# Four experts with a fixed place instead of three, and another order of the blocks, in a two-part transformer kernel

## What is computed

```python
scores = jax.nn.sigmoid(jnp.dot(h, w_router, preferred_element_type=F32))     # 256 x 64
...
_, idx = lax.top_k(jnp.where(expert_mask, biased, -jnp.inf), TOP_K)            # 8 of 64 experts a token
gate = gate / jnp.sum(gate, axis=-1, keepdims=True) * ROUTED_SCALE
...
y = (jax.nn.silu(xb @ w_gate[e]) * (xb @ w_up[e])) @ w_down[e]                 # 1024 -> 256 -> 1024
return y.astype(F32) * w_b[:, None]
```

## Time and profile before

| | us |
|---|---|
| median of three runs | 1319.2 |
| lowest and highest | 1319.04, 1322.58 |
| the profiled execution | 1320.62 |
| its span (first to last instruction) | 1318.8 |
| TensorE busy | 1273.8 (97%) |
| weight loads of TensorE | 796.1 (60%) |
| DVE, ACT, POOL busy | 778.5, 328.0, 147.7 |
| HBM read | 353.73 MB |

### The profile page before, as it was taken

How to read it: one execution, slowest core, us unless ns; L and a number is a source line. 1 busy time by engine, 2 the same in 40 slices (tenths; PEclk the granted TensorE clock), 3 DMA queues, 4 the chain that set the end, 5 groups by cost and what they waited for, 6 DMA issues and landing times.

```text
span 1318.8 us, 20435 instructions
## 1 busy us (share of the span) xinstructions
PE 1273.8 (97%) x7816; PEld 796.1 (60%) x7840; DVE 778.5 (59%) x1404; ACT 328.0 (25%) x658; POOL 147.7 (11%) x133
## 2 busy tenths in 40 slices
PE   9999999999999999999999999999999989999996
PEld 8667675875879566686686765744434434444431
DVE  1235589778789668968878574634444433444432
ACT  2144311201211251110122152322222222222221
POOL 1125500000011332000000902000000000000000
PEclk9999999999999999999999999999999999999998
DMA  9941154654533346675673414599999999999995
GB/s 380 363 157 35 65 192 164 250 225 174 206 128 130 133 187 234 251 304 209 261 301 147 163 62 178 220 421 410 420 420 421 420 422 420 421 420 421 420 421 236
DMA packets 51221, 356.48 MB, mean 270 GB/s; under 512 B 5936, under 2 KB 6208, under 8 KB 9536
## 3 DMA queue, kind: packets, MB, share of 16 engines
q1 hardware_dynamic: 45456, 321.45, 60.5%
q0 software_dynamic: 5392, 32.05, 6.6%
q10 hardware_dynamic: 288, 1.80, 0.3%
HBM read 353.73 MB, written 1.05 MB: 269 GB/s over the span
## 4 chain that ended last, share of the span: by engine, by line
PE 83%; DMA 6%; DVE 6%; SPq 2%; issue 2%; ACT 1%; DVEq 0%; ACTq 0%
PE ps L1094 14%; PE ps L1085 13%; PE ps L1637 11%; PE ps L1666 5%; PE ps L1567 4%; PE ps L861 4%; PE ps L1375 4%; PE ps L1617 4%; PE ps L1042 4%; DMA y_rows<-in_stream 3%; DMA ring<-in_stream 3%; PE ps L944 2%; PE ps L1024 2%; SPq L745 2%; PE ps L1368 2%; PE ps L965 2%
## 5 line engine op out<-in xcount | busy, mean ns | idle before, releaser
L1809 ACT ACTIVATE x_rows<-masked_and_probs 128x1024 bf16<-128x1024 f32 x72 | 76.1, 1057 | 243.0 <-DVE masked_and_probs L3146 175.4
L3146 DVE SCALAR_TENSOR_TENSOR masked_and_probs<-ps,small,gate_rows 128x512 f32<-128x512 f32 x48 | 33.8, 746 | 113.5 <-PE ps L1666 113.5
L1809 ACT ACTIVATE qk_tiles<-ps 128x512 f32<-128x512 f32 (+7 forms) x58 | 30.2, 522 | 256.4 <-PE ps L1085 248.4
L1085 PEld LDWEIGHTS ps<-xT,ring 128*128 128x128 f32 x768 | 87.7, 192 | 4.9 <-issue 4.9
L1085 PE MATMUL ps<-xT,ring 128*128 128x128 f32 x768 | 88.8, 275 | 0.8 <-issue 0.8
L1094 PE MATMUL ps<-ring,qk_tiles 128*128 128x512 f32 x192 | 85.2, 592 | 0.0
L3153 DVE TENSOR_TENSOR masked_and_probs<-masked_and_probs,x_rows 128x1024 f32<-128x1024 f32 x48 | 58.7, 1223 | 41.3 <-ACT x_rows L1809 41.3
L1637 PE MATMUL ps<-ring,vec_rows 128*32 128x512 f32 (+2 forms) x312 | 64.9, 592 | 4.0 <-DMA ring<-in_stream 2.7
L1617 PE MATMUL ps<-x_rows,probT 128*128 128x512 bf16 x264 | 61.1, 379 | 2.0 <-ACT x_rows L1809 0.8
L1567 PE MATMUL ps<-masked_and_probs,mix_rows 128*128 128x256 bf16 (+1 forms) x384 | 61.9, 269 | 0.7 <-ACT v_rows L2152 0.7
L1841 ACT ACTIVATE masked_and_probs<-masked_and_probs,negmax 128x128 f32<-128x128 f32 (+2 forms) x96 | 47.6, 497 | 59.8 <-DVE negmax L2403 52.5
(11 more groups left out here) (557 smaller groups left out, 2664.7 us busy)
## 6 DMA issues: line engine op xcount, KB each, us to landing
ring<-in_stream SPq DMA_DIRECT2D x201, 1024.0 KB, 10.1
qk_tiles<-in_stream SPq DMA_DIRECT2D x38, 1024.0 KB, 25.1
v_rows<-in_ada POOLq DMA_DIRECT2D x12, 1024.0 KB, 5.4
qk_tiles<-in_ada POOLq DMA_DIRECT2D x12, 1024.0 KB, 6.0
vec_rows<-in_stream SPq DMA_DIRECT2D x12, 1024.0 KB, 22.2
par<-in_stream SPq DMA_DIRECT2D x12, 1024.0 KB, 18.7
y_rows<-in_stream SPq DMA_DIRECT2D x12, 1024.0 KB, 20.7
xT<-in_stream SPq DMA_DIRECT2D x12, 1024.0 KB, 22.3
```

Source lines behind the costliest of these rows:

```text
L1085: mm = pe.matmul(ps[:, bank, m * P:(m + 1) * P], weights[:, kk, m * P:(m + 1) * P], tokens[:, kk, :], start=fresh and m == 0 and kk == 0, ...
L1809: return act.activation(dst, src, ACT.Copy, **kw)
```

## The change

One more expert (number 60) gets a fixed place of 96 rows. The places in sum are the same: 60 in 25 blocks, 4 + 3 + 3 + 17 + 33 instead of 3 + 3 + 3 + 19 + 32. Loads 0 to 11, not 0 to 8, are issued ahead of the wait for `s_sched`. One P block becomes an F block, and the order of the blocks is another one.

```diff
-FIXED = 3
+FIXED = 4
 UNIT = 32
 PER_MORE = P // UNIT
-WIDTHS = ((3 * P // 4, FIXED), (P, 3), (3 * P // 4, 3), (P // 2, 19), (P // 4, 32))
+WIDTHS = ((3 * P // 4, FIXED), (P, 3), (3 * P // 4, 3), (P // 2, 17), (P // 4, 33))
...
-BLOCKS = "TFQFPQPFSPPQQMMSPPQPPSQPM"
+BLOCKS = "FQFPFQSFPQPPPMMSQSPPMQQTP"
```

## The result

| | before | after |
|---|---|---|
| median of 12 runs, us | 1320.33 | 1325.06 |
| lowest and highest | 1318.37, 1322.58 | 1323.71, 1326.92 |
| ratio, 95% interval | | 1.0032 (1.0024 to 1.0040) |
| the profiled execution | 1320.62 | 1326.92 |
| its span | 1318.8 | 1325.1 |

The kernel is slower by 4.2 us (3.2 to 5.3). That is just over the 0.3% at which a change counts as seen. Single executions scatter by some 2 us, and the profiled one of after was the slowest of its twelve, so its 6.3 us over the profiled one of before is on the high side. What one trace shows is therefore read for its places, and the timed medians for the sizes.

The account below looks back on a forecast made before the run. The stream of 192 loads of 1 MB, coupled to TensorE by 17 buffers, was taken as the bound. 7.6 us gained by the preload less 10.9 us lost in holes gave +3.3 on 1319.2, so 1322.5 us; range 1318.5 to 1326.5.

Parts of the forecast that it names:

- the start of the sum: Whole kernel: the median before the change, 1319.2 us, to which the forecast added 3.3 us.
- rival 2: From block 1's wait on: TensorE's clock falls and the stream runs dry again; +5.2 us, 1324.4; chance 0.32.
- The likeliest case: Load stream to load 187: preload gain lost in later holes, then no further gap; +2.2 to +3.9 us; chance 0.5.
- the buffers swallow the gain: Block 0: only 21 loads can be issued by 875, engines idle from 872 until load 21 goes at 875.46.
- net term of +3.3 us: Stream up to load 187: 7.6 us gained from the preload, 10.9 us lost again in holes behind it.
- the bound of +2.6: Stream's pace up to load 187: 0.7 us less than +3.3 if the 0.8 us of old stops is taken out.
- does it run without a gap?: Block 1 on: TensorE waits 4.0 us for load 22, yet the stream keeps 0.9 us of cover at load 31.
- Rival 1, the gain stays: Load stream: its end moves with its earlier start; 7.6 us less, 1311.6 us; chance 0.08.
- Rival 3, a shorter wait in the loop: Loop's second half: short wait, clock stays up, 2.3 us of the tail go; 1321.2 us; chance 0.1.
- The end of the schedule: Closing blocks Q, Q, T, P: TensorE 2.8 us later at the loop's second half, still waits 5.6 us; hidden.
- The rule on early transfers: Loads ahead of the schedule: by issuing early alone, three loads are worth 7.6 us; it ignores buffers running out.

Follow-up runs that it names:

- e1: Changed kernel with 9 loads ahead of the schedule instead of 12, its new order and places kept; +1.5 us against the kernel before.
- e7: Kernel before with only its first two blocks exchanged, F ahead of T; +2.6 us against the kernel before.
- e3: Changed kernel with 9 loads ahead and the old order of blocks (T first, block 10 an F), so new places only; +0.8 us against the kernel before.
- e4: Changed kernel with four more matmuls, result unused, in TensorE's wait for load 22 in block 1; +2.9 us against the kernel before.
- e5: Kernel before with 16 buffers for the experts' loads instead of 17; +2.5 us against the kernel before.
- e9: Kernel before with 6 loads ahead of the schedule instead of 9; +6.9 us against the kernel before.
- e2: Changed kernel with 12 loads ahead kept but the old order of blocks (T first, block 10 an F); +9.8 us against the kernel before.
- e6: Changed kernel with 16 buffers for the experts' loads instead of 17; +9.5 us against the kernel before.

## Why the prediction came out as it did

**The end.** Forecast 1322.5 us (+3.3), range 1318.5 to 1326.5; measured 1325.06. The range held. Of the 2.6 us between 1322.5 and 1325.06, 1.1 are the start of the sum: the three runs of before had a median of 1319.2, the twelve 1320.33. The ratio's +4.2 us lies between the forecast (+3.3) and rival 2 (+5.2), and its interval, 3.2 to 5.3, holds both, so the time alone does not tell them apart. The trace does: the clock fell and the stream stumbled near 902 and 953, which are rival 2's signs. The likeliest case, at 0.5, had neither; rival 2 had 0.32. The range held because it was wide enough for both.

**Holds: the buffers swallow the gain.** Reckoned were 21 loads by 875, load 21 at 875.46 with the engines idle from 872; it went at 875.67, idle from 873. Reckoned was a net term of +3.3 us. The runs that have that hole alone gave +1.5 (e1) and +2.6 (e7). Their own traces can be read too, from block 0's start to the landing of load 187: 437.6 us in before, 440.1 in e1 and 440.6 in e7, so 2.5 and 3.0 more. (e3, which has no such hole, has 438.9: single traces scatter by about as much as that.) The term was rather too big, though 3.3 lies inside e7's interval. Its mechanism held, and the size is nearer to the bound of +2.6 that the prediction gave for a pace without the old stops: in e1 load 21 landed at 879.4 and load 187 at 1296.4, 2.512 us a load and not 2.517. Why the time of e1 is lower still stays open; e1 and e7 differ in everything behind the first block, and their intervals overlap.

**Failed: "does it run without a gap?"** This step answered that 0.9 us of cover was left in block 1. The wait it named was right, 4.0 us reckoned and 4.14 found. What it lacked was a fallen clock, which it left to rival 2, and the clock fell: 5.12 us for the half, a stumble at 902, one at 953. The forecast added nothing for this step. By e4 the clock's share is 1.3 us; rival 2 had 1.9 for it, a little high.

Could have told it? They had two waits: one of 5.24 us in which the clock fell, one of 2.71 us in which it did not. The length of the wait alone does not decide between such cases, as other traces of this study show:

```profile
911.22 1.03 PE L1666 MATMUL ps<-con,probT 128*32 128x512 f32 x1 [2.62 <-DMA ring<-in_stream]
...
1071.70 0.62 PE L1639 MATMUL ps<-ring,vec_rows 128*32 128x512 f32 x2 [3.19 <-DMA ring<-in_stream]
```

The first is e5: within a wait of 2.62 us the clock fell (0.84 over 910 to 911, 0.50 behind it, and the first record takes 1.03 us). The second is e3: through 3.19 us it stayed at 1.00. In e9 a wait of 4.13 us ended at full clock, and the clock fell 0.9 us behind it. But all of the 21 waits of 3.8 us or more in the stretch of the experts, over the eleven traces, have the low clock in them or within 1 us behind them. So a wait of 4 us deserved more than the 0.32 of rival 2; from the two waits of the earlier trace rows alone it could only be guessed.

**Where the rest is.** The changed kernel's +4.2 less the +1.5 of e1 is 2.7 us, which is what the three loads ahead cost in the new order. Of that, e4 gives 1.3 us to the clock. Of the other 1.4 the dip near 951 that is left in e4 is 0.7 us, by its two slices (270 and 262 GB/s for 420). It goes with the wait itself: TensorE is 4 us later from block 1 on, and e1, without that wait, has no dip there. The last 0.7 us are inside the intervals, and no run gives them a place.

**Rival 1, the gain stays,** fell in e2, e6 and in the changed kernel. **Rival 3, a shorter wait in the loop,** didn't come about: it was 5.8 us, reckoned 5.6.

**The end of the schedule** was foreseen to be hidden. The waits ahead of the loop are 21.7 - 5.8 = 15.9 us, reckoned 15.5, and TensorE still stands waiting for load 187. That the sum fits is partly luck. The wait of about 6 us at the T block isn't there; from 1230 to 1280 the longest is 3.81 us, and the rest is spread over five shorter ones. The clock fell in that wait too (0.66 over 1250 to 1255), under the cover of the last wait.

**The rule on early transfers.** The Trainium skill, DMA: Bandwidth & Descriptors, section "Rules for kernel authors", says to issue early. The runs bear that out up to 9 loads ahead (e9), and not from 9 to 12 (e1 against after, e2 against e3). For a transfer into idle engines the row of before had 4.8 us, and load 21 of after, issued at 875.67, took 4.8 us as well. Load 22 of after was issued at 876.20 and let TensorE go on at 883.05, 6.85 us later with load 21 issued 0.53 us ahead of it: 4.8 + 2.5 - 0.5 is 6.8. The section "Bandwidth" of the same page of the Trainium skill has 6.15 us for 1 MB, issued from GpSimd; an estimate with that figure gives 8.1 us. The measured 6.85 us decides for 4.8.

## What to carry to other kernels

Moving transfers into an idle stretch ahead gains only as much as there are buffers that come free soon enough afterwards; count the loads that can be issued up to each release, at the consumer's pace, and look for the next place where the stream must stop. The first consumer behind the idle stretch should free many buffers early, and a new wait of the matrix engine of some 4 us should be priced in the forecast with the lower clock behind it: here all 21 waits of 3.8 us or more had it, and some shorter ones did. What a fallen clock costs depends on the place: 1.3 us in block 1, where buffers came free late by it, and nothing that could be seen near 1251, ahead of a longer wait. One size changed downward (one buffer less, three loads fewer) shows on which side of the knee a kernel stands.

## What the runs showed that I had not expected

In e2 the 32 records behind the wait of 5.12 us took 6.45 us, 2.9 more than at full clock; rival 2 of the prediction had 2.3 for such a half. Another wait followed in block 2, again with a lower clock behind it, and the time came out 3 us above the sum. And a preload that pays 2.3 us a load from 6 to 9 costs 9.0 us for the next three when the order isn't changed with it (e2 against e3).
